# Two-layer encoder trunk on one core: products of zeros in TensorE's waits, and a new order of attention, stage changes, routing and gather

## The reference

```python
x = x + swa_sink_attention(rmsnorm(x), ...)   # 16 heads, 4 KV heads, chunks of 64, window 128
x = x + swiglu(rmsnorm(x), ...)               # width 2816
x = x + gated_deltanet(rmsnorm(x), ...)       # 16 value heads, chunked delta rule
x = x + moe_swiglu(rmsnorm(x), ...)           # top 2 of 8 experts, width 3584
return rmsnorm(x)
```

## Time and profile before

| | us |
|---|---|
| median of 3 runs | 1856.39 (1855.88 to 1856.95) |
| the profiled execution's own time | 1854.62 |
| its span, first to last instruction | 1852.8 |
| TensorE busy | 1714.4 (93%) |
| VectorE busy | 1315.3 (71%) |
| ScalarE busy | 1060.3 (57%) |
| GpSimd busy | 172.1 (9%) |

### The profile page before, as it was taken

One profiled execution on the slowest core, in us unless ns is written; L12 is line 12 of the kernel. 1 busy time (PEld: TensorE's weight loads), 2 busy tenths in 40 slices (PEclk: granted clock), 3 DMA queues, 4 the chain that ended last, 5 costly groups with the idle time before them and its releaser, 6 DMA issues.

```text
span 1852.8 us, 23270 instructions
## 1 busy us (share of the span) xinstructions
PE 1714.4 (93%) x9044; PEld 1461.5 (79%) x9044; DVE 1315.3 (71%) x1055; ACT 1060.3 (57%) x1028; POOL 172.1 (9%) x115
## 2 busy tenths in 40 slices
PE   7679999798999987768999999999999999999996
PEld 6569999687878876757888888888888888888885
DVE  4534444356584847237989989889899898898986
ACT  3633343353544543316767767777677777776773
POOL 0000000006262625200000000000000000000000
PEclk9679999799999998868999999999999999999998
DMA  9017555242132200127999999999999999999993
GB/s 351 25 30 247 182 181 183 68 137 92 46 96 88 69 1 1 56 92 282 362 342 364 361 351 354 371 341 355 347 361 359 350 344 379 339 360 345 361 361 123
DMA packets 155421, 437.89 MB, mean 236 GB/s; under 512 B 9280, under 2 KB 40416, under 8 KB 155360
## 3 DMA queue, kind: packets, MB, share of 16 engines
q1 hardware_dynamic: 155360, 437.03, 65.5%
HBM read 435.95 MB, written 1.05 MB: 236 GB/s over the span
## 4 chain that ended last, share of the span: by engine, by line
PE 84%; DVE 9%; ACT 4%; issue 2%; DMA 0%; POOL 0%; DVEq 0%; SPq 0%; POOLq 0%; ACTq 0%
PE bank L1258 24%; PE bank L1260 23%; PE bank L1259 23%; DVE wlo L806 2%; PE bank L1573 2%; PE bank L1562 2%; PE bank L1675 1%; ACT whi L501 1%; DVE TT L1065 1%; PE bank L1686 1%; PE bank L1685 1%; PE bank L1580 1%; DVE T L1043 1%; PE bank L1607 1%; ACT sc L548 0%
## 5 line engine op out<-in xcount | busy, mean ns | idle before, releaser
L1145 DVE TENSOR_TENSOR wlo<-raw,whi 128x2048 fp32r<-128x2048 f32 x336 | 767.6, 2291 | 120.2 <-ACT whi L721 116.9
L721 ACT CAST whi<-raw 128x2048 fp32r<-128x2048 f32 x336 | 643.9, 1917 | 264.2 <-PE bank L1260 264.2
L1258 PE MATMUL bank<-whi,xhi 128*128 128x512 f32 (+1 forms) x1584 | 578.3, 365 | 19.3 <-DVE wlo L1145 6.4
L1260 PE MATMUL bank<-whi,xlo 128*128 128x512 f32 (+1 forms) x1584 | 570.7, 360 | 0.0
L1259 PE MATMUL bank<-wlo,xhi 128*128 128x512 f32 (+1 forms) x1584 | 570.3, 360 | 0.0
L1258 PEld LDWEIGHTS bank<-whi,xhi 128*128 128x128 f32 x1584 | 303.3, 192 | 64.7 <-issue 10.6
L1260 PEld LDWEIGHTS bank<-whi,xlo 128*128 128x128 f32 x1584 | 302.9, 191 | 44.5
L1259 PEld LDWEIGHTS bank<-wlo,xhi 128*128 128x128 f32 x1584 | 303.6, 192 | 42.1
L806 DVE TENSOR_TENSOR wlo<-raw,whi 128x2048 fp32r<-128x2048 f32 x75 | 186.0, 2484 | 153.8 <-ACT whi L501 153.7
L501 ACT CAST whi<-raw 128x2048 fp32r<-128x2048 f32 x75 | 142.9, 1909 | 86.4 <-PE bank L1260 85.6
L1258 PE MATMUL bank<-whi,ehhi 128*128 128x512 f32 x448 | 178.1, 398 | 1.8 <-DVE ehlo L1160 1.8
(11 more groups left out here) (256 smaller groups left out, 1718.2 us busy)
## 6 DMA issues: line engine op xcount, KB each, us to landing
raw<-in_moe_w_gate_dram SPq DMA_DIRECT2D x112, 1024.0 KB, 6.7
raw<-in_moe_w_up_dram SPq DMA_DIRECT2D x112, 1024.0 KB, 6.4
raw<-in_moe_w_down_dram SPq DMA_DIRECT2D x112, 1024.0 KB, 6.6
raw<-in_dn_w_in_dram SPq DMA_DIRECT2D x24, 1024.0 KB, 5.1
raw<-in_ffn_w_gate_dram SPq DMA_DIRECT2D x11, 1024.0 KB, 5.3
raw<-in_ffn_w_up_dram SPq DMA_DIRECT2D x11, 1024.0 KB, 5.3
raw<-in_ffn_w_down_dram SPq DMA_DIRECT2D x11, 1024.0 KB, 5.0
raw<-in_dn_w_o_dram SPq DMA_DIRECT2D x8, 1024.0 KB, 5.2
```

Source lines behind the costliest of these rows:

```text
L721: act.copy(slot(whi, n, SPLIT), slot(raw, n, RAW)).then_inc(hi_ready, 1)
L1145: dve.tensor_tensor(slot(wlo, n, SPLIT), slot(raw, n, RAW), slot(whi, n, SPLIT).bitcast(F32), ALU.subtract).then_inc(lo_ready, 1)
L1258: pe.matmul(ps, lhs_hi, wh, start=start, stop=False)
L1260: return pe.matmul(ps, lhs_lo, wh, start=False, stop=stop)
```

## The change

- `keep_clock(count, bank)`: TensorE multiplies a tile of zeros (`spare`) into a bank that is free, 128x512, `count` times: 10 and 14 at the start, 10 + 3 + 3 + 8 in attention, 5 and 14 in the delta rule's last group, 14 and 4 at its end, 10 + 5 + 4 + 6 in routing.
- Attention: k and v are projected first; 24 of the 40 head transposes stand between the panels of the projection; VectorE copies two of the last four. Sums of exponentials are VectorE's, the scaling of three of four chunks is GpSimd's. VectorE's list has the first score tile behind one panel less. The output projection of the first half of the tokens starts when two chunks are attended (`w_o_half`).
- Changes of stage: one panel less is split before them, the last row panel is ordered by halves of the columns (`last_rows`), so that half of X is added earlier, and products wait for each pair of xlo tiles.
- Delta rule: the gate products are 24 of 256 columns with 32 weights, behind the first panel of the projection, with a transpose back; the gate sums stand two panels later.
- Routing: logits from X itself, with the gain in the router's weights and `rs` applied to the difference of logits; H is made by blocks; the ranks are two products; selection stands before the gates and before the count; three whi and the first wlo of the experts stand in the routing.
- Gather: `pick` (8 products, 512 columns) to `picked`, ScalarE's copy, then eight transposes.

The core of the diff:

```diff
+        QKV_COLS = (2 * 512, 0, 512)
+        for n0 in QKV_COLS:
+            wide(w_qkv, n0)
...
+            for n in range(NCH - 1):
+                s3 = sc[n][:, :].rearrange("p (j k) -> p j k", j=PAIRS)
+                pool.wait_ge(sem("sums_ready"), n + 1)
+                pool.tensor_tensor(s3, s3, rsum[n].unsqueeze(2).broadcast_to([P, PAIRS, P]), ALU.mult)\
+                    .then_inc(sem("probs_ready"), 1)
...
+            probs_T(0)
+            exps(2)
+            probs_T(1)
+            attended_hi(0)
+            exps(3)
...
-            hi_panels.upto(P_FFN + 2)
+            hi_panels.upto(P_FFN + 1)
...
             split_hi(2)
-            sum_squares()
-            act.wait_ge(sem("rs_ready"), 3)
-
             act.wait_ge(phase_b_params, 32)
             act.copy(hhi[:, 0:256], wba[:, :]).then_inc(sem("wba_hi"), 1)
+            sum_squares()
+            hi_panels.upto(P_IN + 2)
+            act.wait_ge(sem("baT_psum"), 1)
...
-                if part == 0:
+                if part == 1:
...
+                    dve.wait_ge(*((panel_used, used) if h else (sem("half_rows"), nth)))
...
-            lo_panels.upto(P_WO + 2)
+            for f in (7, 9):
+                dve.wait_ge(sem("head_psum"), f + 1)
+                dve.tensor_copy(head_dst(f), head_src(f)).then_inc(sem("head_sb_late"), 1)
...
+                link(dve.tensor_reduce(ssum[n], s3, AX_X, ALU.add))
                 link(dve.tensor_tensor(ssum[n], ssum[n], es[n], ALU.add))
-                link(dve.reciprocal(rsum[n], ssum[n]))
-                dve.tensor_tensor(s3, s3, rsum[n].unsqueeze(2).broadcast_to([P, PAIRS, P]), ALU.mult)\
-                    .then_inc(sem("probs_ready"), 1)
+                i = dve.reciprocal(rsum[n], ssum[n])
+                if n < NCH - 1:
+                    i.then_inc(sem("sums_ready"), 1)
+                else:
...
+            lo_panels.upto(P_WO + 2)
+            summed(0)
             largest(2)
-            for n in range(NCH):
-                normalised(n)
-                if n == 0:
-                    largest(3)
-                else:
-                    attended_lo(n - 1)
-            attended_lo(NCH - 1)
-            lo_panels.upto(P_FFN + 2)
...
+            lo_panels.upto(P_FFN + 1)
+            add_y(P_FFN, 1)
...
-            norm(3, gain3[:, :], H3)
-            dve.wait_ge(sem("h2hi_ready"), 1)
-            dve.tensor_tensor(h2lo, H3, h2hi.bitcast(F32), ALU.subtract).then_inc(sem("h2lo_ready"), 1)
...
+            elo(P_MOE, 0)
+            dve.wait_ge(sem("logit_psum"), 1)
...
             select(0)
...
+            elo(P_MOE + 1, 0)
             gathered_lo(0)
-            for i in range(HEAD):
+            elo(P_MOE + 2, 0)
...
+            def keep_clock(count, o_):
+                for _ in range(count):
+                    pe.matmul(o_, spare[:, 0:P], spare[:, :], start=True, stop=True)
+
+            pe.wait_ge(sem("spare_ready"), 1)
+            keep_clock(10, bank[7])
...
+                n = wide_panel(n, 0, outs)
+                if c:
+                    pe.wait_ge(sem("qkv_ready"), c)
+                    heads_T(*((0, 2) if c == 1 else (2, 6)))
+                n = wide_panel(n, 1, outs)
...
+            scores(0, 0, 4)
+            pe.wait_ge(sem("qkv_ready"), 3)
+            heads_T(6, 10)
+            pe.wait_ge(sem("head_sb"), 8)
+            pe.wait_ge(sem("head_sb_late"), 2)
+            scores(0, 4, PAIRS)
+            for c in range(1, NCH):
+                scores(c, 0, PAIRS)
+            keep_clock(10, bank[0])
+            for c in range(2):
                 probs_T(c)
+                keep_clock(3, bank[2 + c])
                 attend(c)
+            pe.wait_ge(sem("score_sb"), NCH)
+            keep_clock(8, bank[4])
+            pe.wait_ge(sem("oTlo_ready"), 2)
+            for c in range(2):
+                w_o_half(c, 0)
+                probs_T(2 + c)
+                attend(2 + c)
+            w_o_half(2, 0)
             pe.wait_ge(sem("oTlo_ready"), NCH)
-            for c in range(4):
-                n = row_panel(n, lambda k, b: xT(2 * c + k, b), c == 0, c == 3)
+            for c in range(3):
+                w_o_half(c, 1).then_inc(panel_used, 1)
...
+            def beta_decay():
+                pe.wait_ge(sem("xlo_ready"), 12)
+                pe.wait_ge(sem("wba_lo"), 1)
+                o_ = bank[4][0:2 * VH, 0:SEQ]
                 for k in range(KT):
-                    a_, l_ = xT(k, b)
-                    s_ = slice(k * 32, (k + 1) * 32)
-                    pe.matmul(o_, a_, hhi[:, s_], start=k == 0, stop=False)
-                    pe.matmul(o_, a_, hlo[:, s_], start=False, stop=False)
-                    i = pe.matmul(o_, l_, hhi[:, s_], start=False, stop=k == KT - 1)
-            i.then_inc(sem("ba_psum"), 1)
+                    s_, x_ = slice(k * 2 * VH, (k + 1) * 2 * VH), slice(k * SEQ, (k + 1) * SEQ)
+                    pe.matmul(o_, hhi[:, s_], xhi[:, x_], start=k == 0, stop=False)
+                    pe.matmul(o_, hlo[:, s_], xhi[:, x_], start=False, stop=False)
...
+                if i == 1:
+                    beta_decay()
+                if i == 2:
+                    beta_decay_T()
+                if i == 7:
...
+                if g == GROUPS - 1:
+                    pe.wait_ge(sem("z_scaled"), GROUPS)
+                    keep_clock(5, bank[6])
...
+                if g == GROUPS - 1:
+                    keep_clock(14, bank[6])
...
+            pe.wait_ge(sem("outputs_added"), 2 * (GROUPS - 1))
+            keep_clock(14, bank[6])
             outputs_T(GROUPS - 1)
+            keep_clock(4, bank[6])
             pe.wait_ge(sem("onlo_ready"), 2 * GROUPS)
             for i in range(4):
                 output(GROUPS - 1, i, bank[4 + 2 * (i % 2) + i // 2])
 
-            transposed(H3, 3)
-            pe.wait_ge(sem("hTf_ready"), 4)
-            for b in range(TB):
-                for k in range(KT):
...
+            keep_clock(10, bank[1])
+            pe.wait_ge(sem("masks_ready"), 1)
+            pe.matmul(bank[0][:, 0:3 * NE], tb_("tri"), own, start=True, stop=False)
+            pe.matmul(bank[0][:, 0:3 * NE], tb_("ones"), earlier, start=False, stop=True).then_inc(sem("rank_psum"), 1)
+            keep_clock(5, bank[1])
...
+            def pick(tokens):
                 pe.wait_ge(sem("sel_ready"), tokens + 1)
                 for h in range(2):
+                    s_ = slice(h * 512, (h + 1) * 512)
+                    for b in range(TB):
+                        pe.matmul(bank[6 + h], sel[:, b, :], h2hi[:, b, s_], start=b == 0, stop=False)
+                        i = pe.matmul(bank[6 + h], sel[:, b, :], h2lo[:, b, s_], start=False, stop=b == TB - 1)
+                    i.then_inc(sem("pick_psum"), 1)
...
-                gate_up_half(B_MOE + G3, it)
+                gate_up_half(B_MOE + G3, it, 0, 2)
                 if not last:
                     pe.wait_ge(sem("ehlo_ready"), it * ECH + 3)
-                    gather(it + 1)
+                    pick(it + 1)
+                gate_up_half(B_MOE + G3, it, 2, 4)
+                if not last:
+                    gather(it * 2 + 2)
```

387 lines of the change are left out of this document (229 added, 158 removed).

## The result

The changed kernel takes 1782.9 us (median of 4 runs, 1781.01 to 1786.47) against 1856.14 us (4 runs, 1855.69 to 1856.95): ratio 0.9607, 95% interval 0.9591 to 0.9624. The forecast was 1793 us with a range of 1779 to 1810: side and range held, and the kernel is 10 us better than the forecast. The profiled execution took 1781.98 us, its span 1780.2 us.

A forecast was written before the change was run, and what follows sets the result against it. The prediction took TensorE, with 84% of the chain, to bound the kernel; terms of 21.5, 14.7, 4.2, 16.7 and 5.9 sum to 63.0 us off 1854.62, giving 1791.6, with 1.8 for the median 1793 us; range 1779 to 1810.

The forecast's parts named there:

- Start and attention: Kernel start through attention to the first dense product: 21.5 us less, bounds 15 and 24.
- The step from scores to probabilities: In attention, first scores to first probabilities: 12.5 us after the change, where it took 10.5 before.
- no such stall of a small one: In attention, GpSimd might hold up VectorE's small maximum, at worst 7 us; the traces showed no such case.
- Dense layer to delta rule: Last dense product to the end of the delta rule's projection: 14.7 us less, bounds 11 and 18.
- The stall: Delta rule's projection: TensorE waits 4.2 us for ScalarE's bank-freeing copy, queued behind the gate chain and one whi.
- Last group: Delta rule's last group: zeros gain 1.2 us, as VectorE sets the pace; bounds with the end 0 and 5.5.
- The end itself: End of the delta rule's last group: zeros gain 3.0 us, all of it on the path.
- Routing: Last output product to first expert product: 39.3 to 24.3 us, plus 1.7 of low clock, 16.7 less; bounds 13 and 18.5.
- Expert loop: Seven turns of the expert loop: a shorter gather saves 0.85 us each, 5.9 us; bounds 0 and 6.
- Zeros do not hold the clock: Rival on the zero products at all their places: 13 to 14 us lost, 1807 us, chance 0.14.
- Rivals 2 to 4: Attention stays a ping-pong, 1800, chance 0.13; transfers hold the expert loop, 1799, 0.07; late expert panels, slower, 1881, 0.02.
- Rival 5: Better than forecast: clock high throughout and a shorter stall at the gates, 1780 us, chance 0.09.

## Why the prediction was right, point by point

- **Start and attention (21.5; 22.75 measured with the dense layer).** No gain at the start: first product at 16.59 instead of 15.73, and the low clock from 17.5 to 20.9 in spite of 24 zeros. The first score tile stood on VectorE at 60.49 (forecast 58.4), the first output product at 83.06 (82.5), the last ended at 111.92 (111.0), the first dense product came at 114.64 (114.2). Of the 2 us late at the scores GpSimd, at 1.90 instead of 2.4 us, made 0.5 good. The step from scores to probabilities was added up to 12.5 us where its four terms give 12.3. Against the GpSimd part the prediction saw "no such stall of a small one" in the traces; the kernel before had the same stall in large ones (2.57 to 2.89 us for a 128x512 product that took 0.69 once, in the delta rule), and attention escaped it by its order and by GpSimd's 1.90 us.
- **Dense layer to delta rule (14.7; 15.6).** The stall was forecast at 4.2 us on ScalarE's queue and measured 3.48, at the place and by the engine named, with the low clock behind it (331.5 to 338.4); changing the order of that queue left 1.42 us of it and no spell. The beta products were 2.8 us, and in their old form cost 4.6.
- **Last group (1.2; 4.5): the term that was mis-sized.** The step was "in the last group VectorE, not TensorE, sets the pace soon after, so 1.2". The kernel of before with zeros alone shows 3.0 us there, and the changed one 4.5. My reading, which no run takes apart further: in the group TensorE's own transposes and small products lie on the chain between VectorE's steps, so that each is waited for at the price of its clock; VectorE's busy time was 47.6 us of 87.4, which left room for it. The bound of 5.5 for group and end together was too low as well (7.6). The end itself was right: 3.0 forecast, 3.2 measured.
- **Routing (15.0 to the first expert product; 15.3).** The order on VectorE was read rightly, and that nothing on TensorE is waited for. The term for the low clock behind it was 1.7 and measured 3.2: before, it fell again in the first turn (862.9 to 869.7), which I had left out. By the run without zeros in routing this gain is the shorter stage's, not theirs.
- **Expert loop (5.9; 6.3).** A turn is 0.90 us shorter (forecast 0.85), put back by the old gather alone.
- **Left out:** 1.2 us in groups 1 to 3 and 0.6 in the tail, no instruction of which changed. The 1.2 are in the first group: one spell of 3.4 us in both kernels, before at 484.0 and now at 389.6. All that was left out or sized too low adds up to the 9.6 us between the span's 72.6 and the forecast 63.0.
- **The rivals.** "Zeros do not hold the clock" is refuted by two runs; its price (13 to 14 us) was near the 10 us that zeros are worth. It had a point in routing, where they are worth nothing. The rows it was weighed by were read too simply: the scores began at the high level, which lasted to 60.8, and the clock did not rise behind products of 512 columns in each stage. It rose at 84.7 among attention's 128-column products, at 139.3 among 256-column ones and at 344.1 after transposes alone. Rivals 2 to 4 didn't come. Rival 5, better than forecast, is nearer in size (1780 against 1782.9), but the gain over the forecast came by half through the last group and the first turn (3.4 and 1.5 of 9.6 us), and the stall was only 0.7 us shorter. That the time fell inside the range is in part luck, since no term foresaw these 4.9 us.

## What to carry to other kernels

Price a wait of TensorE with what the low clock costs afterwards; products of zeros in four waits, which ended at most 1.7 us before the data, gave 7.6 us, and 25 that left a gap of 5 us gave nothing. Before filling a wait, look at whose queue it stands in: twice the awaited engine did work that nobody was waiting for (a whi and a logarithm, a low part and a wlo), and two changes of order there gave 10 us, as much as all the zeros. And an edit's own stage says what it does; a total also contains spells of low clock elsewhere, up to 5 us here, and some of them come with no edit at all.

## What the runs showed of the hardware

- The low clock was granted also in stretches in which TensorE was busy throughout (3.28 of 3.30 us from 442.2, 3.27 of 3.30 from 722.1). In the 3.4 us before each fall it was busy for 1.68 and 1.69 us, with waits of at most 1.16 us: no long wait was needed. The changed kernel had no spell in either place, at the same work; the kernel before had one at the first (484.0 to 487.5). What decides isn't shown.
- A VectorE product of two SBUF inputs, 128x512, took 0.69 us when it began before GpSimd's, and up to 2.90 us when GpSimd was reading SBUF already; with one input in PSUM it took 0.68 us beside it. No run takes GpSimd's part of the delta rule away, so what this costs the kernel is open.
- A product of 32 columns takes as long as one of 128: 0.11 us from start to start at the high level, and 0.11 for the gather's 128 columns.
- Between 311.5 and 314.0 TensorE did the 16 transposes into the delta rule at a granted clock of 1.00, and the clock fell only at 331.5, in the stall that began at 329.0; the transposes into the dense layer (111.9 to 114.7) the same. The rule weighed in the prediction (Trainium skill, TensorE: Matmul & The Clock Gate, section "Part 4: PE-mode transpose") would have them count for less; here that cost nothing.
